# Prompt attention of a stick-breaking layer: the causal mask moved from a matmul into the scan and a select

## What is computed

```python
# 16 heads of 64; query block of 128 rows, keys 0 .. end of the block
z = jnp.einsum('bqhd,bkhd->bhqk', qb, kb) * scale
mask = kpos[None, :] < qpos[:, None]                      # strictly causal
log_one_minus = jnp.where(mask, jax.nn.log_sigmoid(-z), 0.0)
after = lax.cumsum(log_one_minus, axis=3, reverse=True) - log_one_minus
a = jnp.where(mask, jnp.exp(jax.nn.log_sigmoid(z) + after), 0.0)
out = jnp.einsum('bhqk,bkhd->bqhd', a, vb)
```

## Time and profile before

| | us |
|---|---|
| median of three runs (2163.28 to 2167.41) | 2166.84 |
| the profiled execution, its own time | 2166.64 |
| its span, first to last instruction | 2164.9 |
| PE busy in the span | 2107.9 (97%) |
| DVE, ACT, POOL busy | 1257.7, 880.0, 728.1 |

### The profile page before, as it was taken

One profiled execution on the slowest core, in us unless ns is written; L12 is line 12 of the kernel. 1 busy time (PEld: TensorE's weight loads), 2 busy tenths in 40 slices (PEclk: granted clock), 3 DMA queues, 4 the chain that ended last, 5 costly groups with the idle time before them and its releaser, 6 DMA issues. The chain is left out here.

```text
span 2164.9 us, 33739 instructions
## 1 busy us (share of the span) xinstructions
PE 2107.9 (97%) x13316; PEld 1994.0 (92%) x13316; DVE 1257.7 (58%) x1861; ACT 880.0 (41%) x1640; POOL 728.1 (34%) x453
## 2 busy tenths in 40 slices
PE   5999999999999999999999999999999999999998
PEld 5999999999899999998999988799999999988875
DVE  5036021000777888767565647688887878833565
ACT  4222211222777777755443122244333333423343
POOL 2335433443744554435655310003343434100000
PEclk9999999999999999999999999999999999999999
DMA  5115422655655555537666543221222222464654
GB/s 183 49 63 172 143 86 84 175 158 157 156 144 140 136 129 137 124 112 218 173 176 198 184 134 99 69 79 61 80 71 80 71 80 71 170 216 135 214 179 163
DMA packets 305651, 285.15 MB, mean 132 GB/s; under 512 B 51078, under 2 KB 270422, under 8 KB 305494
## 3 DMA queue, kind: packets, MB, share of 16 engines
q1 hardware_dynamic: 292432, 252.88, 40.3%
q10 hardware_dynamic: 10822, 21.99, 2.8%
q0 software_dynamic: 2240, 8.13, 1.0%
HBM read 203.59 MB, written 79.35 MB: 131 GB/s over the span
## 5 line engine op out<-in xcount | busy, mean ns | idle before, releaser
L294 PE MATMUL p_psB<-hT_lo,w_hi 128*128 128x364 f32 x888 | 295.3, 333 | 2.4 <-issue 2.4
L294 PE MATMUL p_psB<-hT_hi,w_lo 128*128 128x364 f32 x888 | 292.9, 330 | 0.0
L294 PE MATMUL p_psB<-hT_hi,w_hi 128*128 128x364 f32 x888 | 292.4, 329 | 0.0
L1185 DVE TENSOR_TENSOR_SCAN p_rest<-p_rest 128x896 f32<-128x896 f32 (+7 forms) x128 | 214.8, 1689 | 85.2 <-ACT p_rest L1108 85.2
L958 POOL TENSOR_TENSOR p_weights<-p_weights,p_rest 128x895 f32<-128x895 f32 (+7 forms) x128 | 160.3, 1258 | 207.8 <-DVE p_rest L1185 207.8
L582 ACT ACTIVATE p_line<-p_psB 128x364 f32<-128x364 f32 x108 | 51.3, 475 | 374.0 <-PE p_psB L294 374.0
L2729 DVE TENSOR_TENSOR p_w_lo<-p_w_raw,p_w_hi 128x512 fp32r<-128x512 f32 (+1 forms) x168 | 160.7, 961 | 52.2 <-ACT p_w_hi L2523 52.1
L294 PEld LDWEIGHTS p_psB<-hT_lo,w_hi 128*128 128x128 f32 x888 | 167.8, 189 | 3.2 <-issue 2.6
L294 PEld LDWEIGHTS p_psB<-hT_hi,w_hi 128*128 128x128 f32 x888 | 167.7, 189 | 0.0
L294 PEld LDWEIGHTS p_psB<-hT_hi,w_lo 128*128 128x128 f32 x888 | 167.6, 189 | 0.0
L2523 ACT ACTIVATE p_w_hi<-p_w_raw 128x512 fp32r<-128x512 f32 (+1 forms) x186 | 139.2, 772 | 65.7 <-DVE p_rows L2748 35.1
(11 more groups left out here) (386 smaller groups left out, 6078.2 us busy)
## 6 DMA issues: line engine op xcount, KB each, us to landing
p_w_raw<-in_w_down SPq DMA_DIRECT2D x66, 512.0 KB, 3.9
p_w_raw<-in_w_up SPq DMA_DIRECT2D x44, 512.0 KB, 4.8
w_raw<-in_w_in SPq DMA_DIRECT2D x40, 512.0 KB, 3.8
hid_scratch<-p_rows ACTq DMA_DIRECT2D x22, 545.0 KB, 2.9
p_kT<-k_hi_scratch SPq DMA_DIRECT2D x32, 256.0 KB, 4.4
p_kT<-k_lo_scratch SPq DMA_DIRECT2D x32, 256.0 KB, 5.2
w_raw<-in_w_gate SPq DMA_DIRECT2D x16, 512.0 KB, 4.9
p_raw_v<-in_cache_sb_v SPq DMA_DIRECT2D x8, 1024.0 KB, 6.3
```

Source lines behind the costliest of these rows:

```text
L294: last = nc.tensor.matmul(out[:, 0:CH], stat[:, slot, w], mov[:, k, c], start=(at == 0), stop=(at == 3 * KT - 1))
L1185: nc.vector.tensor_tensor_scan(src, src, src, 1.0, ALU.mult, ALU.bypass).then_inc(s("scanned"), 1)
```

## The change

The mask matmul is gone, with the tensors `unit_r`, `mask` and `plain` and PE's wait for them. The last piece of a block is scored by two matmuls and both sigmoids are those of the unmasked scores.

The factor 1 for masked keys now comes from the scan. Its second input was the same `rest`, not used by the second operation (`bypass`); it is now `floor`, a tensor of 1024 columns that is 0 except in the last 128, where it is 1 above and on the diagonal. The scan computes max(rest · state, floor): the state stays 1 over the masked keys, which it meets first, and is the product from there on. A block of n keys takes the last n columns of `floor`, backwards.

The weight 0 for masked keys comes from POOL: ahead of each block's multiply an `affine_select` over the last 128 columns of `wt`, which writes 0 where masked. It waits for the block's sigmoid(z) alone, ahead of the wait for the scan; the multiply waits for the scan and for the select's own signal `cleared`. POOL makes `floor` ahead of the loop by a memset and a select, and DVE waits for it ahead of the first scan.

```diff
--- before.py
+++ after.py
@@ -827,10 +827,8 @@
         aT = f("p4_aT", [P, 2, 4, 2, 2 * P], F32R)
         ytmp = f("p4_ytmp", [64, 2 * P])
         gates = f("p4_gates", [P, GST, CH])
-        unit_r = f("p4_unit", [P, P], F32R)
         yb = small("p4_yb", [64, YST, 2 * P])
-        mask = f("p4_mask", [P, 2, 2 * P], F32R)
-        plain = f("p4_mask_plain", [P, 3, P])
+        floor = f("p4_floor", [P, SEQ])
         psD = [ps_open, ctx.enter_context(nc.psum_tensor("p4_psD1", [P, 512], F32)),
                ctx.enter_context(nc.psum_tensor("p4_psD2", [P, 512], F32))]
         psZ = ctx.enter_context(nc.psum_tensor("p4_psZ", [P, 2, 512], F32))
@@ -953,8 +951,11 @@
                 pool.sem_clear(ODD)
                 def weigh(b):
                     n = (tile_of(b) + 1) * P
+                    pool.wait_ge(s("beta"), ZBEFORE[b + 1])
+                    nc.gpsimd.affine_select(out=wt[:, b % 6, n - P:n], in_=wt[:, b % 6, n - P:n], compare_op=ALU.is_gt, fill=0.0, base=0,
+                                            pattern=[[-1, P]], channel_multiplier=1).then_inc(s("cleared"), 1)
                     pool.wait_ge(s("scanned"), b + 1)
-                    pool.wait_ge(s("beta"), ZBEFORE[b + 1])
+                    pool.wait_ge(s("cleared"), b + 1)
                     nc.gpsimd.tensor_tensor(wt[:, b % 6, 0:n - 1], wt[:, b % 6, 0:n - 1], rest[:, b % 4, 1:n],
                                             ALU.mult).then_inc(s("weights"), 1)
 
@@ -976,14 +977,10 @@
                                             ALU.subtract).then_inc(s("q_lo"), 1)
 
                 ring.start_pool(pool, 1)
-                nc.gpsimd.memset(plain[:], 0.0).then_inc(s("mask_made"), 1)
-                pool.wait_ge(s("mask_made"), 1)
-                nc.gpsimd.affine_select(out=plain[:, 1, :], in_=plain[:, 1, :], compare_op=ALU.is_gt, fill=MASKED, base=0,
-                                        pattern=[[-1, P]], channel_multiplier=1).then_inc(s("mask_made"), 1)
-                pool.wait_ge(s("mask_made"), 2)
-                nc.gpsimd.tensor_scalar(mask[:, 0, :], plain[:, 1:3, :].rearrange("p a c -> p (a c)"), 1.0, 0.0, ALU.mult, ALU.add)
-                nc.gpsimd.tensor_scalar(mask[:, 1, :], plain[:, 0:2, :].rearrange("p a c -> p (a c)"), 1.0, 0.0, ALU.mult, ALU.add)
-                nc.gpsimd.tensor_scalar(unit_r[:], ident[:], 1.0, 0.0, ALU.mult, ALU.add).then_inc(s("mask_made"), 1)
+                nc.gpsimd.memset(floor[:], 0.0).then_inc(s("floor_made"), 1)
+                pool.wait_ge(s("floor_made"), 1)
+                nc.gpsimd.affine_select(out=floor[:, SEQ - P:], in_=floor[:, SEQ - P:], compare_op=ALU.is_gt, fill=1.0, base=0,
+                                        pattern=[[-1, P]], channel_multiplier=1).then_inc(s("floor_made"), 1)
                 pool.wait_ge(kept("q_ahead"), 16)
                 split(1)
                 for e in range(2):
@@ -1016,12 +1013,8 @@
                     n = max(n, 2 * P)
                     out = psZ[:, z % 2, 0:n]
                     stat = qT[:, hb, i * P:(i + 1) * P]
-                    masked = c + 512 > i * P
                     nc.tensor.matmul(out, stat, kT[:, hb, 1, c:c + n], start=True, stop=False)
-                    last = nc.tensor.matmul(out, stat, kT[:, hb, 0, c:c + n], start=False, stop=not masked)
-                    if masked:
-                        at, which = (0, 0) if i % 4 == 0 else (i * P - c - P, 1)
-                        last = nc.tensor.matmul(psZ[:, z % 2, at:at + 2 * P], unit_r[:], mask[:, which, :], start=False, stop=True)
+                    last = nc.tensor.matmul(out, stat, kT[:, hb, 0, c:c + n], start=False, stop=True)
                     last.then_inc(s("z"), 1)
 
                 def turn(k):
@@ -1073,7 +1066,6 @@
                 pe.wait_ge(kept("opened"), 1)
                 pe.sem_inc(s("group"), 1)
                 fill(PART, FIRST - PART)
-                pe.wait_ge(s("mask_made"), 3)
                 pieces = [(b, part) for b in range(2 * LEAD) for part in range(len(parts(tile_of(b))))]
                 cuts = [FIRST + BETWEEN * x // len(pieces) for x in range(len(pieces) + 1)]
                 for x, (b, part) in enumerate(pieces):
@@ -1182,7 +1174,8 @@
                     n = (i + 1) * P
                     dve.wait_ge(s("nb"), ZBEFORE[b + 1])
                     src = rest[:, b % 4, n - 1::-1]
-                    nc.vector.tensor_tensor_scan(src, src, src, 1.0, ALU.mult, ALU.bypass).then_inc(s("scanned"), 1)
+                    least = floor[:, SEQ - 1:SEQ - 1 - n:-1] if n < SEQ else floor[:, SEQ - 1::-1]
+                    nc.vector.tensor_tensor_scan(src, src, least, 1.0, ALU.mult, ALU.max).then_inc(s("scanned"), 1)
 
                 def split_lo(k):
                     w, g = UNITS[k]
@@ -1199,6 +1192,7 @@
                         dve.wait_ge(kept(f"y_stored{w % YST}"), 16 * (w // YST))
                     nc.vector.tensor_tensor(yb[:, w % YST, :], psY[0:64, 0:2 * P], ytmp[:, :], ALU.add).then_inc(s("y"), 1)
 
+                dve.wait_ge(s("floor_made"), 2)
                 for b in range(2 * LEAD):
                     scan(b)
                 for k, (w, g) in enumerate(UNITS):
```

## The result

The changed kernel takes 2169.98 us (median of 11 runs, 2166.93 to 2172.96) where the kernel before took 2166.84 (also 11 runs, 2163.28 to 2167.92). The ratio is 1.0019 with a 95% interval of 1.0012 to 1.0027: slower by some 3 to 4 us. The profiled execution took 2172.06, 2 us over its kernel's median, so lengths of whole stretches in it are the less favourable ones. Of 15.4 us of matmuls taken off PE nothing is left in the time, and more than that was added elsewhere. 0.1% is 2.2 us in all that follows; "ratio" is always against the kernel before on the same chip.

What follows compares the result with a forecast made beforehand. It took PE to be full, with two chains through POOL and DVE level with it. Shifts by groups of heads, 1.7 + 0.2 - 0.6 - 2.0 - 1.7, made -2.4 us: 2164.4 us forecast, range 2159 to 2172.

Steps and rivals of the forecast that it cites:

- d: Added delay of POOL's multiply behind its block's scan, from the new select; taken as 0.10 us, between 0 and 0.38.
- (a): First heads, to 577 us: four unhidden selects on a POOL without a break, and the next head's chain; +1.7 us.
- The two narrow places: In a head, PE's 1024-key transposes closely follow POOL's multiply (0.2 us to spare), and PE needs DVE's sum of y.
- The rival that all 15.4 would show: Chains of the stage looser than read, so all the mask matmuls' time comes out: 2151.4 us; chance 0.03.
- Mask matmul, scan, preparation: 128 matmuls of 0.12 us leave PE, 15.4 in all; scan length unchanged; preparation ahead of the loop gains or loses nothing.
- The multiply then starts 0.09 later: POOL's multiply follows the select's end by 0.09 us, so stands 0.18 behind the scan instead of 0.08.
- (b): Four heads from 577 to 680 us: four selects in series, +4d, less three masks, -0.36; +0.04 a head, +0.2 us.
- (c): From 680 us to the next head's chain: five mask matmuls come free, -0.6 us.
- (e): Three last heads: nothing gained at the 1024-key transposes, then five, five and four masks free; -1.7 us.
- (d): Seven heads to 863 us: +2d on PE's wait for the sum of y, less four masks; -0.28 a head, -2.0 us.
- Paid in full, d = 0.38: Rival: nothing of the select is hidden behind each scan; +8.5 us, 2175.3; chance 0.13, with values from 2168 on.
- Costs nothing: Rival: the select adds nothing to the chain, d near 0; -5.6 us, 2161.2; chance 0.18.

## Why the prediction was wrong, and where it was right

It said 2164.4 with "no change" likeliest, so 2.4 us faster; the median is 2169.98 and the ratio's interval lies between 0.12 and 0.27% slower. That the median is inside the range of 2159 to 2172 is no merit of the sum: the range was made to take in a delay d up to 0.3, and d came out at half of that; what carried the time up is in (a) and the third head.

*What bounds the stage: right.* The two narrow places were there; 15.4 us of matmuls gave 5 (kernel before without the mask matmul). By the prediction's own terms a kernel without mask matmul and without select comes to -5.6 less the 1.7 of (a), some -7; with the old scan that kernel measured -5.0 (interval -3.0 to -6.9), with the new one -5.0 as well and, with the two waits the other way round, -7.1 (-4.6 to -10.0). Its head near 725 is 25.13, 25.24 and 25.12 where 25.55 - 0.48 = 25.07 was due. The rival that all 15.4 would show is excluded.

*Mask matmul, scan, preparation: right.* The undisturbed 896-key scan is 2.02 as before, the heads equal in both forms. The preparation took 0.95 + 0.29 us on POOL, and what is behind it starts at 528.07, 9.5 us ahead of the first score.

*The select's end: right.* It was to end 0.09 behind the scan; it ends 0.08 to 0.10 behind.

*"The multiply then starts 0.09 later": wrong.* This is the first mis-sized term. Rows 11 have two gaps behind an instruction that the next one waits for (both wait for `mask_made`): the select is 0.15 behind the memset, the conversion 0.10 behind the select. The prediction took the smaller, and the multiply behind `cleared` goes by the larger; why the two differ no run shows. It starts 0.14 to 0.15 behind the select, 0.24 behind the scan. So d is 0.15 to 0.16, not 0.10, which is the point that the prediction itself named as the one from which the change loses. A head at 731 goes by that: 25.55 + 2 x 0.16 - 0.48 = 25.39, measured 25.43, where the forecast said 25.3. With d = 0.16 in its formula, the sum is about 0 (-5.6 + 32 x 0.16 + 0.5, the last for the three last heads), not -2.4. Of the 0.16, 0.06 is the longer gap of this wait. Whether the select's wait written ahead of the scan's would take it off wasn't run.

*(a), the first heads to 577, +1.7: wrong, the largest error.* It counted four selects of 0.38 on a POOL without a break. By the second head's multiply the shift is 4.6, of which 1.27 was there at the start, so +3.3; and the third head, which the prediction counted in (b) at +0.04, then has a stall of its own. By medians the selects of the first two heads cost 3.5 us and those of the third 2.6. Two things failed. The first is the price of 0.29 + 0.09 for each select on a late POOL: it starts at any moment, also under a scan, and the selects of the lines above took 1.75, 1.22 and 2.41 us. The scan it waits out isn't all its own cost, though, since in the third head the multiply meets it just as well without that head's selects; what these add is 1.0 us. The second is that the sum had no term for the clock: an estimated 1.7 of the third head's 2.6 us, and 2 to 4 of the 6 us of the first three heads, are PE at half clock. In the first head what part is the select's wait stays open, since the kernel with memsets waits there and falls to half clock as well.

*(b), +0.04 a head: wrong.* After the third head the heads take 26.06, 26.11 and 25.92 where they took 25.50, 25.53 and 25.39: 0.56 more each. With d = 0.16 the forecast's own terms give 4 x 0.16 - 0.36 = 0.28. The four selects in series are there: POOL goes from the end of the 384-key scan to the end of the 1023-element multiply in 14.2 us in place of 13.5. It is the three masks' 0.36 that doesn't come back in full.

*(c) to (e), -4.3: right in sign, less than half the size.* The shift falls from 9.0 to 7.3 from the sixth head to the last, -1.7; with d = 0.16 the prediction's own terms give -0.6 in (c), -1.1 in (d) and -1.2 in (e), -2.9; what is missing beyond that no run separates.

*The rivals.* "Paid in full, d = 0.38" came out on the right side, but not by its mechanism: 0.20 of the select's length is hidden, as its end shows. In full it would have cost the chain 12.2 + 1.9 = 14.1 us; the select costs 9, and by the medians 6 of them in the first three heads, which that sum doesn't single out. "Costs nothing" is excluded by the 0.42%. The Trainium skill has it on that page (SBUF — State Buffer, "Summary: rules for kernel authors") that with two SBUF inputs on DVE and a reading GpSimd operation the second to issue "fully blocks" until the first finishes. Taken to mean that its whole length comes after the first, that doesn't hold here: the select of 0.29 ends 0.09 after the scan.

*Of the signs that were to be looked for*, the select's end, the longer 1024-key scan and the wait named POOL came true. The head of 25.55 near 650 (it is 26.06), the multiply 0.18 behind its scan (0.23) and PE's busy time near 50 (46.41 from 600 to 650) did not. "The forecast is wrong if the time to 577 doesn't grow" looked in the wrong direction: in the trace it grew by twice what was forecast.

## What to carry over

Where two engines lock one another out, an added operation is priced by where it ends and by what must wait for it, never by its busy time; and an operation that only writes may be put where one that reads may not. If the profile has two values for the same kind of gap, work the sum with both before giving it a direction: here 0.10 and 0.15 us lay on the two sides of the point at which the change loses. Read the heads in which an engine is already late by themselves, and take PE's clock into the sum where PE waits longer than before: by the medians three heads of sixteen cost more than the other thirteen, and a good part of that was the clock. And before a collision is called an operation's doing, look at the trace of a kernel without it: in the third head the collision was there as well.

## What the runs showed of the hardware that was not expected

The order in which two waits of one operation are written changed its start, both on semaphores of other engines. With the late event's wait written last (beta, then the scan) the multiply stood 0.15 behind the scan; with the late event's wait first and the long-met one last (the scan, then beta) 0.08. The multiply behind its own engine's select, whose wait is also the last written, stands at the 0.15. The trace doesn't show why.

An operation of POOL whose record begins 0.04 us ahead of a scan's can still lose to it: the select of 602.75 against the scan of 602.79, and the multiply of 600.00 against the scan of 600.04 in the kernel with selects in two heads, where the scan took its undisturbed 2.27 and the multiply 3.89. In both, the operation of POOL ahead of it ended just as the scan began. At 0.08 us ahead POOL won: the multiply of 595.88 took its 1.77 and the scan of 595.96 3.84, in the kernel without a select.

TensorE, in a stage otherwise at a clock of 1.00, was at half speed in part of the windows around waits of 3.35 and 2.04 us (granted clock 0.69 and 0.66), and at 1.00 in the same place of the third head behind waits of 1.90, 1.69 and 1.31. In the first head the clock fell to 0.66 behind a wait of 2.48 in a kernel that has no select.
